# RWKV chunk stage: the raw key product kept once by ScalarE, both off-diagonal parts cut out of it by GpSimd

## What is computed

```python
def frame_step(state, inp):
    r_t, w_t, k_t, v_t, kk_t, b_t = inp          # b_t is kk_t * a_t
    sa = jnp.einsum('bhvk,bhk->bhv', state, -kk_t)
    state = (state * w_t[:, :, None, :] + sa[..., None] * b_t[:, :, None, :]
             + v_t[..., None] * k_t[:, :, None, :])
    return state, jnp.einsum('bhvk,bhk->bhv', state, r_t)
...
_, o = lax.scan(chunk_step, state0, xs)
```

## Time and profile before

| | us |
|---|---|
| median of 3 runs | 2108.09 |
| lowest and highest | 2106.91, 2111.71 |
| the profiled execution's own time | 2114.92 |
| its span, first to last instruction | 2113.4 |
| PE busy in the span | 2004.0 (95%) |
| DVE busy | 1227.6 (58%) |
| ACT busy | 940.3 (44%) |
| POOL busy | 204.2 (10%) |

### The profile page before, as it was taken

One profiled execution on the slowest core, in us unless ns is written; L12 is line 12 of the kernel. 1 busy time (PEld: TensorE's weight loads), 2 busy tenths in 40 slices (PEclk: granted clock), 3 DMA queues, 4 the chain that ended last, 5 costly groups with the idle time before them and its releaser, 6 DMA issues. The chain is left out here.

```text
span 2113.4 us, 32315 instructions
## 1 busy us (share of the span) xinstructions
PE 2004.0 (95%) x12489; PEld 1574.1 (74%) x12489; DVE 1227.6 (58%) x1672; ACT 940.3 (44%) x1219; POOL 204.2 (10%) x193
## 2 busy tenths in 40 slices
PE   7998889999999999998999999998999899988998
PEld 5865447888888888887888878786577578777776
DVE  3356476532333344547666566888368854547887
ACT  2125545532222331234656565775253633416774
POOL 0010100000000000004001110012112210003111
PEclk9999999999999999999999999999999999999999
DMA  9108024240442540117777887995320000248996
GB/s 250 38 21 306 14 60 130 60 135 26 120 125 60 184 160 1 50 42 237 278 271 273 283 283 274 393 392 233 89 80 30 13 1 1 81 177 235 387 384 231
DMA packets 221483, 338.62 MB, mean 160 GB/s; under 512 B 50421, under 2 KB 135573, under 8 KB 221374
## 3 DMA queue, kind: packets, MB, share of 16 engines
q1 hardware_dynamic: 214238, 316.78, 44.2%
q0 software_dynamic: 7136, 20.34, 2.6%
HBM read 309.07 MB, written 26.95 MB: 159 GB/s over the span
## 5 line engine op out<-in xcount | busy, mean ns | idle before, releaser
L1884 DVE TENSOR_TENSOR moe_pass_wL<-moe_pass_w,moe_pass_wH 128x2048 fp32r<-128x2048 f32 (+1 forms) x144 | 303.3, 2112 | 110.8 <-ACT moe_pass_wH L1805 110.7
L1805 ACT ACTIVATE moe_pass_wH<-moe_pass_w 128x2048 fp32r<-128x2048 f32 (+1 forms) x144 | 254.9, 1773 | 127.1 <-PE PS L652 86.0
L1884 DVE TENSOR_TENSOR hm_pass_wL<-hm_pass_w,hm_pass_wH 128x2048 fp32r<-128x2048 f32 x60 | 135.7, 2287 | 29.5 <-ACT hm_pass_wH L1805 29.4
L650 PE MATMUL PS<-moe_pass_wL,moe_pass_xgH 128*128 128x512 f32 (+1 forms) x384 | 147.8, 385 | 3.4 <-DVE moe_pass_wL L1884 2.1
L652 PE MATMUL PS<-moe_pass_wH,moe_pass_xgH 128*128 128x512 f32 (+1 forms) x384 | 143.2, 373 | 0.0
L651 PE MATMUL PS<-moe_pass_wH,moe_pass_xgL 128*128 128x512 f32 (+1 forms) x384 | 143.2, 373 | 0.0
L650 PE MATMUL PS<-xnT_low,ffn_upH 128*128 128x512 f32 (+2 forms) x360 | 138.9, 386 | 0.3 <-PE PS L652 0.3
L652 PE MATMUL PS<-ffn_xH,ffn_upH 128*128 128x512 f32 (+2 forms) x360 | 138.7, 385 | 0.0
L651 PE MATMUL PS<-ffn_xH,ffn_up_low 128*128 128x512 f32 (+2 forms) x360 | 138.7, 385 | 0.0
L1805 ACT ACTIVATE hm_pass_wH<-hm_pass_w 128x2048 fp32r<-128x2048 f32 x60 | 112.1, 1910 | 16.4 <-DMA hm_pass_w<-in_exp_w_up 7.0
L1110 DVE TENSOR_TENSOR ffn_hT<-ffn_sg,PS 128x512 f32<-128x512 f32 x22 | 15.1, 688 | 160.9 <-PE PS L652 160.9
(11 more groups left out here) (883 smaller groups left out, 4716.7 us busy)
## 6 DMA issues: line engine op xcount, KB each, us to landing
moe_pass_w<-in_moe_w_down SPq DMA_DIRECT2D x40, 1024.0 KB, 6.8
moe_pass_w<-in_moe_w_gate SPq DMA_DIRECT2D x32, 1024.0 KB, 7.1
moe_pass_w<-in_moe_w_up SPq DMA_DIRECT2D x32, 1024.0 KB, 8.1
hm_pass_w<-in_exp_w_gate SPq DMA_DIRECT2D x40, 512.0 KB, 7.5
hm_pass_w<-in_exp_w_up SPq DMA_DIRECT2D x40, 512.0 KB, 7.1
hm_pass_w<-in_exp_w_down SPq DMA_DIRECT2D x40, 512.0 KB, 7.3
od_W<-in_od_w_in SPq DMA_DIRECT2D x12, 1024.0 KB, 10.5
moe_pass_w<-in_moe_w_gate SPq DMA_DIRECT2D x16, 768.0 KB, 7.0
```

Source lines behind the costliest of these rows:

```text
L650: nc.tensor.matmul(out, lh, rl, start=start, stop=False)
L1805: nc.scalar.activation(wH[:, i % S, 0:n], w[:, i % R, 0:n], ACT.Copy).then_inc(s["high"], 1)
L1884: nc.vector.tensor_tensor(wL[:, i % S, 0:n], w[:, i % R, 0:n], f32(wH[:, i % S, 0:n]), ALU.subtract) \
```

## The change

The gram of At and Bt is made once. In the first section its take moves from DVE to ACT, which copies it unmasked into `M1`. DVE now makes `MA` from that copy, inside the take of the second gram, between the mask to UA and the sum Y. GpSimd gets work in the stage: per tile it makes `M2` from the raw M1 (mask 3), waits until DVE has read the raw M1 (`raw_used`), and then masks M1 in place (mask 2). The second making of the gram, in the middle section, goes, and with it DVE's two masks there. PE waits for all 8 of GpSimd's instructions (`off`) before the first transpose of step 4.

```diff
             for t in tiles:
-                made_m[t] = gram("V", (), t, At, Bt, lambda ps, t=t: masked(ps, t, (MA, 0)))
+                made_m1[t] = made_m2[t] = gram("A", (), t, At, Bt, kept(M1, t))
                 made_tok[t][0] = by_token(t, 0)
 
                 def take_u(ps, t=t):
                     masked(ps, t, (UA, 1)).then_inc(opened, 1)
+                    nc.vector.wait_ge(taken["A"], taken_by("A", made_m1[t]))
+                    nc.vector.tensor_tensor(MA[:, t], M1[:, t], bcast(masks[:, 0].unsqueeze(1), [P, HH, P]), ALU.mult).then_inc(raw_used, 1)
                     nc.vector.wait_ge(opened, t + 1)
                     return nc.vector.tensor_tensor(Y[:, t], UA[:, t], bcast(C.ident[:, :].unsqueeze(1), [P, HH, P]), ALU.add)
-                made_u[t] = made_y[t] = gram("V", (), t, Bt, At, take_u)
+                made_m[t] = made_u[t] = made_y[t] = gram("V", (), t, Bt, At, take_u)
...
                 m = mul("A", (made_u[t], made_m[t]), UB[:, t], MB[:, t], kept(MA, t))
-                made_m1[t] = made_m2[t] = gram("V", (), t, At, Bt, lambda ps, t=t: masked(ps, t, (M1, 2), (M2, 3)))
...
+            off_at = len(jobs)
             for Moff, made_off in ((M1, made_m1), (M2, made_m2)):
...
+                @block.gpsimd
+                def _(pool):
+                    for t in tiles:
+                        pool.wait_ge(taken["A"], taken_by("A", made_m1[t]))
+                        nc.gpsimd.tensor_tensor(M2[:, t], M1[:, t], bcast(masks[:, 3].unsqueeze(1), [P, HH, P]), ALU.mult).then_inc(s["off"], 1)
+                        pool.wait_ge(raw_used, t + 1)
+                        pool.wait_ge(s["off"], 2 * t + 1)
+                        nc.gpsimd.tensor_tensor(M1[:, t], M1[:, t], bcast(masks[:, 2].unsqueeze(1), [P, HH, P]), ALU.mult).then_inc(s["off"], 1)
...
+                        if n == off_at:
+                            pe.wait_ge(s["off"], 2 * NT)
```

More of the change, by code:

```diff
@@ L4119, in rwkv @@
             slot = [made_g[t] % 4 * 2 for t in tiles]
-            with stage(nc, "rw_chunks", "made taken_v taken_a opened steps_v states_made states rows_made rows outs_made outs") as (block, s):
+            with stage(nc, "rw_chunks", "made taken_v taken_a opened raw_used off steps_v states_made states rows_made rows outs_made outs") as (block, s):
                 PS, taken, opened = C.PS, dict(V=s["taken_v"], A=s["taken_a"]), s["opened"]
+                raw_used = s["raw_used"]
+                @block.gpsimd
[6 more added lines that the diff above has]
+                        nc.gpsimd.tensor_tensor(M1[:, t], M1[:, t], bcast(masks[:, 2].unsqueeze(1), [P, HH, P]), ALU.mult).then_inc(s["off"], 1)
                 @block.tensor
```

## The result

| comparison (each against runs of the kernel before that belong to it) | changed kernel, median (runs) | before, median (runs) | ratio, 95% interval |
|---|---|---|---|
| first | 2113.43 us (20) | 2108.86 us (20) | 1.0017 [1.0010, 1.0025] |
| second (`e5_changed_again`) | 2110.84 us (11) | 2112.13 us (22) | 0.9996 [0.9985, 1.0007] |
| third (`e10_changed_third`) | 2108.92 us (12) | 2110.51 us (23) | 0.9997 [0.9985, 1.0009] |
| the kernel before against itself (`e12_before_itself`) | 2109.24 us (12) | 2111.95 us (17) | 0.9996 [0.9983, 1.0009] |

The forecast was 2108.9 us, 0.8 above the median of the three runs of before that were known then (2108.09), with a range up to 2113.5; the first measurement, 2113.43, lies just inside. By its own ratio it is 3.6 us (0.17%) slower (the medians lie 4.6 apart), and the two repetitions contradict that.

A forecast was written before the change was run, and what follows sets the result against it. PE was taken to bound the middle section, a PE-DVE latency loop the first. First section +4.21 and middle -3.38 gave +0.8 us on 2108.09, so 2108.9 us; range 2105.0 to 2113.5.

The forecast's parts named there:

- Middle section: Four grams leave PE's path between the squarings there, saving 3.38 us; DVE's dropped masks give nothing.
- The collision: First section: GpSimd and two-SBUF-input DVE instructions block each other, so the second tile's squaring starts 4.21 us later.
- p: Time of one GpSimd mask in the first section, taken as 1.27 us.
- the repeated mask: GpSimd reading 128 mask columns repeated for four heads might lengthen its masks; long-masks rival, chance 0.10.
- Loop: First section's time per tile, from one sum Y to the next: 3.52 us in place of 2.23.
- The sum: Whole stage: first section's +4.21 less the middle section's 3.38, giving +0.8 us.
- the case without a collision: Rival: in the first section GpSimd and DVE pass each other, loop 2.72, net -1.7 us; chance 0.18.
- The wait for `off`: PE's wait for GpSimd ahead of step 4's first transposes costs nothing.
- The clock: Rival: PE's clock falls through first-section gaps, costing 1.5 us on the squarings behind, net +2.3; chance 0.15.

The follow-up runs named there:

- e5_changed_again: The changed kernel measured once more, unaltered, against the kernel before; 2110.84 us against 2112.13, ratio 0.9996.
- e10_changed_third: The changed kernel measured a third time, unaltered, against the kernel before; 2108.92 us against 2110.51, ratio 0.9997.
- e12_before_itself, e12: The kernel before, unaltered, measured against its own other runs; 2109.24 us against 2111.95, ratio 0.9996.
- e1: Changed kernel with GpSimd's eight masks held until after DVE's last take of the first section; 2107.30 us against 2109.82, ratio 0.9993.
- e8: Changed kernel with only GpSimd's four masks to M2 in the first section, those to M1 after its last DVE take; one execution, 2110.18 us.
- e4: Changed kernel with the middle section's four grams and eight DVE masks made again; 2113.88 us against 2109.82, ratio 1.0019.
- e9: Kernel before, with only finish_norm moved from ahead of step 4 to behind DVE's middle masks; 2106.76 us against 2110.51, ratio 0.9980.

## Why the prediction was right, step by step

- **Middle section, -3.38.** Measured -3.36. DVE's masks gave nothing, as written.
- **The collision.** p, the time of a GpSimd mask, came out at 1.27 (1268 ns, four masks), so the repeated mask costs nothing extra. Loop 3.51 for 3.52; mask to M1 1.13 behind Y's end, mask to MA 0.55 behind GpSimd's. Fourth Y at 14.38 us from the first gram, 14.42 by the prediction; second squaring without a fall at 14.43, which is +4.16 for +4.21.
- **The sum, +0.83.** In the execution whose clock held, the first transposes come 0.80 us later than before (51.83, 51.03). e1 and e8 confirm the parts by their absence: -1.71 and -1.61 at the same mark for the -1.7 of the case without a collision. In the two executions whose clock fell, the same mark is at +1.76 and +1.88.
- **The wait for `off`.** Never seen: the wait ahead of the first transposes is PE's 1.82 for 1.81 before, still for DVE, and GpSimd's last mask had ended 37 us earlier.
- **The clock.** I gave its fall a chance of 0.15 and a cost of 1.5 us. It fell in the first section in two of three profiled executions (and in e4's), so the chance looks far too small; it cost 0.8 to 1.1, since part of the slow time is spent waiting for DVE. I had not thought of the other half: in those executions the fall behind step 4, worth 1.5, was absent. At M1 the three profiles are at +0.25, +0.36 and +0.80, against a profile of before that has the fall behind step 4. Whether one fall tends to keep the other away, or three profiles happened to look so, is open; all three executions with the first fall lack the second, but so do e1 and e8, which have neither.
- **The time.** The forecast, a ratio of 1.0004, lies below the 1.0017 of the first series and above the 0.9996 and 0.9997 of the next two. By the inverse squares of their intervals the three ratios average 1.0008, +1.6 us, but an average of ratios whose intervals don't all meet says little. What is shown is the stage: -0.1, +0.75 and +0.4 us at the next stage's first matmul in three profiles. Where the first series got its 3.6 us from is not shown; nothing in its own profile holds them, the stage there being 0.1 us shorter than before, and its lower mean clock (e12) goes with a part of them.
- **The range** held by 0.07 us, which is luck. It had allowed 1.4 us for scatter between series. The medians of before alone moved from 2108.86 to 2112.13 between comparisons, which is more than twice that. So the whole time neither confirms nor refutes a sum of +0.8 us; the marks in the trace do.

The Trainium skill ("SBUF — State Buffer", section "SBUF: two separate sides") describes the port pair as an exclusive lock for a whole instruction between GpSimd and a VectorE instruction with two SBUF inputs. The trace agrees, with 1.65 for 1.27 and 1.48 for 0.69, and with 0.69 untouched where one input was PSUM; the one that waited then ended 0.14 us sooner than its free time (1.13 for 1.27, 0.55 for 0.69). The estimate of 1.07 us from the 2.5 cycles an element that the Trainium skill gives as a floor ("GPSIMD Engine Reference", section "2.1 Instruction dispatch") was too low for a whole instruction: 1.27 was measured.

## What to carry to other kernels

Read the loop, not the load: DVE was busy for 80% of the first section, but the mask to MA was free where it stood and cost 0.5 us a tile inside the take that frees a bank pair, and 0.8 more when GpSimd's second mask got in front of it. Before giving GpSimd work beside DVE, list which of DVE's instructions have two SBUF inputs and where each asks for the port; one GpSimd instruction per loop fitted for 0.1 us in all, two cost 0.8 us a loop, and all eight late cost nothing at all. When an engine idles somewhere, look for what it is late with elsewhere: finish_norm, moved into DVE's idle time, gave 1.98 us at the first transposes, more than the edit's own sum. The 7.6 us that the edit freed were not needed for it; the gap that the kernel before already had was enough (e9).

## What was not expected of the hardware

- Two gaps of PE, of 0.80 and 1.41 us, in the 3.51 us loops were followed by a granted clock of 0.50 for some 6 us (1722 to 1728) in two of three executions of the same program; in the third the same gaps and one more of 1.42 left it at 1.00. With 2.71 us loops and gaps of 0.6 to 0.8 (e1, e8, one execution each) it stayed at 1.00.
- Executions of one program pass the marks of a stage within 0.02 us of each other at the same clock, while their whole times spread over 8 to 12.5 us in the series of before. A change of a few us belongs in the trace first and in the medians after.
